# Two transformer blocks on one core: a chunked scan run as a pipeline over pairs of heads, and a last linear turned to rows

## What is computed

```python
def _wkv7_scan(r, w, k, v, a, b):
    def step(S, inp):
        r_t, w_t, k_t, v_t, a_t, b_t = inp
        sa = jnp.einsum('bhvk,bhk->bhv', S, a_t)
        S = (S * w_t[:, :, None, :] + sa[..., None] * b_t[:, :, None, :]
             + v_t[..., None] * k_t[:, :, None, :])
        return S, jnp.einsum('bhvk,bhk->bhv', S, r_t)
...
def _layer(h, ...):
    proj = _rms(h, n1) @ w_in
    z_rwkv, z_fox, z_gate = jnp.split(proj, (RWKV_COLS, RWKV_COLS + FOX_COLS), axis=-1)
    z_prev = jnp.pad(z_rwkv, ((0, 0), (1, 0), (0, 0)))[:, :-1]
    z_rwkv = z_rwkv + (z_prev - z_rwkv) * mu
    y_a = _rwkv7(z_rwkv, ...)        # r, k, v, decay, a, gate from z_rwkv, then the scan
    y_b = _fox(z_fox, q_g, k_g, f_bias)
    ...
    gate, up = jnp.split(_rms(h, n2) @ w_gu, 2, axis=-1)
    return h + (jax.nn.silu(gate) * up) @ w_dn
...
return h[:, N_META:]                 # the meta tokens are dropped
```

## Time and profile before

| | us |
|---|---|
| median of 3 runs | 2893.81 (2892.56 to 2895.17) |
| the profiled execution | 2892.87 |
| its span, first to last instruction | 2890.8 |
| TensorE busy | 2856.2 (99%) |
| VectorE busy | 1735.4 (60%) |
| ScalarE busy | 1223.3 (42%) |
| the scan with the side slots in it (first `sums` to last output of pair 8) | about 1398 to 1757 |
| `down2` | about 2633 to 2891 |

### The profile page before, as it was taken

How to read it: one execution, slowest core, us unless ns; L and a number is a source line. 1 busy time by engine, 2 the same in 40 slices (tenths; PEclk the granted TensorE clock), 3 DMA queues, 4 the chain that set the end, 5 groups by cost and what they waited for, 6 DMA issues and landing times.

```text
span 2890.8 us, 55153 instructions
## 1 busy us (share of the span) xinstructions
PE 2856.2 (99%) x23517; PEld 2629.2 (91%) x23517; DVE 1735.4 (60%) x2522; ACT 1223.3 (42%) x1788; POOL 53.0 (2%) x102
## 2 busy tenths in 40 slices
PE   9999999999999999999999999999999999999999
PEld 8999998888888999899888888899998888889999
DVE  6467757656566444754666665766666566655444
ACT  5345544333333344633433333455453333334343
POOL 1000000000000000000000000000000000000000
PEclk9999999999999999999999999999999999999999
DMA  7666445565555555455434335445555555555553
GB/s 245 199 168 167 156 163 172 177 190 187 188 189 175 190 187 189 153 167 168 118 88 118 102 89 160 132 123 184 180 186 188 182 183 187 189 189 183 182 188 131
DMA packets 370328, 485.21 MB, mean 168 GB/s; under 512 B 12359, under 2 KB 181654, under 8 KB 370150
## 3 DMA queue, kind: packets, MB, share of 16 engines
q1 hardware_dynamic: 362752, 471.55, 51.6%
q0 software_dynamic: 4112, 7.88, 0.9%
q10 hardware_dynamic: 3302, 3.39, 0.4%
HBM read 475.76 MB, written 7.01 MB: 167 GB/s over the span
## 4 chain that ended last, share of the span: by engine, by line
PE 91%; DVE 6%; issue 1%; ACT 1%; DMA 1%; DVEq 0%; SPq 0%; ACTq 0%
PE psum L338 20%; PE psum L344 12%; PE psum L342 12%; PE psum L343 12%; PE psum L340 10%; PE psum L543 6%; PE psum L547 5%; PE psum L545 5%; DVE w_lo L328 2%; PE psum L1796 1%; DVE arena L716 1%; PE psum L1782 1%; DVE arena L704 0%; PE psum L2612 0%; DVE act L791 0%
## 5 line engine op out<-in xcount | busy, mean ns | idle before, releaser
L328 DVE TENSOR_TENSOR w_lo<-w_raw,w_hi 128x1024 fp32r<-128x1024 f32 x728 | 859.0, 1221 | 797.6 <-ACT w_hi L319 797.6
L319 ACT ACTIVATE w_hi<-w_raw 128x1024 fp32r<-128x1024 f32 x728 | 731.4, 1052 | 1161.8 <-PE psum L340 591.5
L338 PE MATMUL psum<-act,w_hi 128*128 128x512 f32 x2816 | 989.6, 394 | 8.9 <-issue 4.5
L342 PE MATMUL psum<-act,w_hi 128*128 128x256 f32 (+2 forms) x3024 | 854.7, 283 | 6.9 <-issue 4.5
L344 PE MATMUL psum<-act,w_lo 128*128 128x256 f32 (+2 forms) x3024 | 855.6, 283 | 0.0
L343 PE MATMUL psum<-act,w_hi 128*128 128x256 f32 (+2 forms) x3024 | 855.6, 283 | 0.0
L340 PE MATMUL psum<-act,w_lo 128*128 128x256 f32 x2816 | 790.7, 281 | 0.0
L338 PEld LDWEIGHTS psum<-act,w_hi 128*128 128x128 f32 x2816 | 529.6, 188 | 136.8 <-DVE w_lo L328 11.2
L342 PEld LDWEIGHTS psum<-act,w_hi 128*128 128x128 f32 (+1 forms) x3024 | 571.6, 189 | 11.3 <-issue 8.3
L344 PEld LDWEIGHTS psum<-act,w_lo 128*128 128x128 f32 (+1 forms) x3024 | 572.2, 189 | 0.0
L343 PEld LDWEIGHTS psum<-act,w_hi 128*128 128x128 f32 (+1 forms) x3024 | 568.4, 188 | 0.1
(11 more groups left out here) (391 smaller groups left out, 1584.8 us busy)
## 6 DMA issues: line engine op xcount, KB each, us to landing
w_raw<-w_in SPq DMA_DIRECT2D x128, 1024.0 KB, 5.7
w_raw<-w_down SPq DMA_DIRECT2D x88, 1024.0 KB, 5.0
w_raw<-w_gate_up SPq DMA_DIRECT2D x88, 1024.0 KB, 5.0
w_raw<-w_gate SPq DMA_DIRECT2D x44, 1024.0 KB, 5.2
w_raw<-w_up SPq DMA_DIRECT2D x44, 1024.0 KB, 5.2
w_raw<-w_out SPq DMA_DIRECT2D x16, 1024.0 KB, 5.0
w_raw<-w_o SPq DMA_DIRECT2D x16, 1024.0 KB, 5.0
w_raw<-w_branch_a SPq DMA_DIRECT2D x8, 1024.0 KB, 5.0
```

The lines of the kernel that those rows point to most:

```text
L319: nc.scalar.activation(w_hi[:, s % 2, 2 * h:2 * h + 2, 0:wd], w_raw[:, s % RAW, 2 * h:2 * h + 2, 0:wd], ACT.Copy).then_inc(hi_ready, 1)
L328: nc.vector.tensor_tensor(w_lo[:, s % 2, 2 * h:2 * h + 2, 0:wd], w_raw[:, s % RAW, 2 * h:2 * h + 2, 0:wd], w_hi[:, s % 2, 2 * h:2 * h + 2, ...
L338: pe.matmul(dst.rearrange("p (h n) -> p h n", h=2), w1, both_parts, start=first, stop=False, skip_group_check=True)
L342: pe.matmul(dst, w1, act_hi[:, k, tok], start=first, stop=False, skip_group_check=True)
```

## The change

- **Chunk steps move.** The chunk steps of pair j - 1 (`chunk_x`, `chunk_u`, `chunk_y`) run between the inverse's steps of pair j. Those of pair 7 stand behind the loop, with slots between them. What they read is doubled or moved for that: `toks_s`, `inv_ts`, `to_mids`, `from_mids` have two copies, and `ar` lies in `z`. The copy of u moves from VectorE to ScalarE.
- **Slots in groups.** Of a step's 31 slots 30 stand in five groups (4, 4, 8, 6, 8) in its first part, and one in the inverse.
- **Gram split.** The product of `bh` with the a half is made only for the blocks that the inverse reads (`near` and `far`: twelve of 32 x 32, four of 64 x 64, per step); its r half (`gram_r`) and the product of `kh` (`gram_k`) come after the inverse.
- **Slots behind the scan.** The loop's end has 8 + 1 + 1 + 2 + 1 + 1 + 2 + 8 = 24 slots where it had 8. `fox_pe`, whose code is the same, is left with 132 slots where it had 148.
- **Last linear by rows.** `rows_pe` takes the activations (128 tokens) as stationary and 512 output features as moving operand. The residual is the first product into each bank (`res` times the identity). `down2_add` and the transposes are gone.
- **Narrow tiles.** The first 8 tiles of `rkv` (r) are made for 258 tokens and the first 8 of `fox` (q) for 256, both 272 before.

```diff
+        def rows_pe(lin, lo_base):
...
+            def residual(s):
+                for b in range(2):
+                    for j in range(4):
+                        pe.matmul(psum[:, 2 * s + b, j * P:(j + 1) * P],
+                                  res[:, 4 * s + j, META + b * P:META + (b + 1) * P], ident,
+                                  start=j == 0, stop=False, skip_group_check=True)
...
+                    if first:
+                        if s < 2:
+                            pe.wait_ge(acc_free, lin.t0 - 2 + 2 * s)
+                        residual(s)
+                    pe.wait_ge(lo_ready, 2 * u + 2)
+                    for b in range(2):
+                        out_rows = psum[:, 2 * s + b, :]
+                        half = slice(META + b * P, META + (b + 1) * P)
+                        for k in range(UNIT_K):
+                            w1, w0 = w_hi[:, s % 2, k], w_lo[:, s % 2, k]
+                            x1, x0 = act_hi[:, 4 * slot + k, half], act_lo[:, 4 * slot + k, half]
+                            pe.matmul(out_rows, x1, w1, start=False, stop=False, skip_group_check=True)
+                            pe.matmul(out_rows, x1, w0, start=False, stop=False, skip_group_check=True)
+                            mm = pe.matmul(out_rows, x0, w1, start=False, stop=last and k == UNIT_K - 1,
+                                           skip_group_check=True)
...
+        R_TOK = slice(META - 2, TOK)
+        def r_tiles(lin, i):
+            return lin is L["rkv"] and isinstance(i, int) and i < 2
...
+        def fox_tok(t):
+            return X if t < 8 else ALL
...
                 dve("n8t")
+                act("raw0")
                 product(4, n8t, n8, "p2")
-                gram(0, 0)
+                if j:
+                    chunk_x(before, 0)
                 dve("ip2")
                 product(5, ip2, i8t, "r1t")
                 act("p2")
                 product(4, p2t, p2, "p4")
-                gram(0, 1)
+                if j:
+                    chunk_u(before, 0)
                 dve("ip4")
                 act("r1t")
                 product(4, r1t, ip4, "s8")
-                gram(1, 0)
+                if j:
+                    act("near")
+                    chunk_y(before, 0)
                 dve("s8t")
                 product(5, nm16, s8t, "v16")
-                gram(1, 1)
+                side(1)
                 act("v16")
                 product(4, v16, s8, "s16")
-                side(1)
+                if j:
+                    chunk_x(before, 1)
                 dve("s16t")
                 product(5, nm32, s16t, "v32", 4)
-                side(1)
+                if j:
+                    chunk_u(before, 1)
                 act("v32")
                 product(4, v32, s16, "s32", 4)
-                side(1)
+                if j:
+                    chunk_y(before, 1)
...
+            side(8)
+            pe.wait_ge(*rd.after(("gram_k", 7)))
+            center(6)
+            chunk_x(7, 0)
+            side(1)
+            chunk_u(7, 0)
+            side(1)
+            chunk_y(7, 0)
+            side(2)
...
-            down_pe(L["down2"], LO_BASE["down2"], lambda s: s > 1 and end_transpose(s - 2))
-            end_transpose(2)
-            end_transpose(3)
+            rows_pe(L["down2"], LO_BASE["down2"])
```

## The result

The changed kernel takes 2920.1 us (median of 4 runs, 2912.9 to 2935.6) where the kernel before takes 2893.2: ratio 1.0096, 95% interval 1.0071 to 1.0121. That is 27 us slower; 2889.9 was forecast, and the range ended at 2901. The profiled execution has 2919.0 us and a span of 2916.9, 26.1 more than before.

A forecast was written before the change was run, and what follows sets the result against it. The kernel was taken as a queue of TensorE work. Narrow tiles -5.3, last linear -1.9, scan -6.3, fox attention's end +8.1 and clock +1.5 sum to -3.9 us, so 2889.9 us; 8 in 10 range 2874 to 2901.

The forecast's parts named there:

- the paragraph on the clock: Fox attention's end: half clock follows the new 5.3 us wait before pair 6's output, +1.5 us, from 0 to 3.5.
- the pair's walk: Scan, inverse and chunk steps: visits -2.7, gaps +0.9, tile changes +0.4, gram +0.1; net -1.3 us a pair.
- wait of 0.35 at x64t: Scan, inverse of a pair: only x0 stands behind v64, so TensorE waits 0.35 us at x64t.
- -8.9 was forecast: First `front` to `ysum`, less the moved slots: scan -6.3 us and `q` tiles -2.6.
- about 311 us: Scan: seven pairs from `sums` to `sums` should take about 311 us where they take 318.
- Rival 3: Inverse of pairs 1 to 7: chain of waits, 0.15 us more per step, 2902; chance 0.21 together with no pipeline gain.
- If a pair takes more than 46 us: Scan: one of the signs named in advance by which the prediction falls.
- the end of the fox attention: Behind the scan: 16 fewer slots for `fox_pe` bring waits of 5.3, 1.7, 0.4 and 1.3 us, less visits; +8.1 us.
- The 1.3 that was to come at the second weight unit: After `branch_first`: ScalarE, running later, and VectorE's part make TensorE wait 1.3 us for the second weight unit.
- the last linear: `down2` and tail: stream -5.4, residual +7.1, transposes in the stream -1.8, tail -1.8; sum -1.9 us.
- rival 2: `down2`: 512 wide matmuls run faster next to each other, 0.216 us, -17 us, 2873; chance 0.11.
- the narrow tiles: r tiles in `rkv` and q tiles in the scan's slots: fewer columns in 384 + 384 matmuls, -5.3 us.

The follow-up runs named there:

- a_spread: The changed kernel with 8 of a pair's 31 slots put back between the inverse's steps, in groups of 2, 3, 2, 2; 2894.0 us, 1.0002.
- b_narrow: The kernel before with the narrow tiles alone; 2890.5 us, 0.9984.
- a_rows128: The changed kernel with 16 of the 18 small matmuls of a product step using all 128 input rows against a fixed table; 2922.2 us, 1.0098.
- a_mid: The changed kernel with two of the eight slots before the inverse moved into the one visit in it, making three there; 2912.6 us, 1.0066.
- a_shift128: The changed kernel with 128 already satisfied waits put once into TensorE's program ahead of the scan; 2912.4 us, 1.0072.
- a_shift64: The changed kernel with 64 already satisfied waits put once into TensorE's program ahead of the scan; 2922.5 us, 1.0094.
- a_again: The changed kernel itself measured once more, as a control; 2924.6 us, 1.0106.

## Why the prediction was right or wrong

**Wrong: the clock.** The step that failed is the paragraph on the clock. It read from rows 8 that a wait of 4.8 us is followed by a stretch at half clock and one of 2.6 us isn't, priced the clock for the one new wait of 5.3 us alone (+1.5), and put it at nothing in the scan. Neither wait of rows 8 stands among small products. In the scan a gap of 1.9 us was enough, with small products around it, and the half clock then lasted 17 and 20 us. The fall of rows 8 lasts 6.8, of which 4.9 lie behind the wait. I had counted the 15 slots that leave the inverse as 2.7 us of visits saved. They also were what kept the clock up. Putting 8 of the 31 back between the steps (a_spread) took off 26 us: some 5 of them are the gaps' own length, the rest, some 21, is the clock.

**Missed: the instruction supply.** The walk of the pair took waits for VectorE and ScalarE only. The kernel before has issue gaps too, five at one line, 2.6 us in all, and one of 0.7 at another; I passed over them. Taking the slots away puts the small products closer together, and the gaps grow to 8.2 us in all (9.6 with that of pair 2). They add 5 to 6 us themselves, and the long falls of pairs 1 and 3 begin with them.

**Near: the pair's walk.** The pairs of the changed kernel at full clock (2, 4, 5 and 6) take 42.8 to 45.3 us, 44.1 on average, where they took 45.4 before. That is the 1.3 that was forecast, but with 0.7 of issue gaps in it, so the walk itself was too pessimistic by some 0.7 us a pair. Its wait of 0.35 at x64t isn't in the trace: in pair 2 x64t starts at 1532.47, 0.03 behind the end of x0. The waits of pair 0 are there, six of 0.4 us instead of four of 0.5. In a_spread the stretch from the first `front` to `ysum`, less 16 slots, is 362.2 against 371.2 before: -9.0, where -8.9 was forecast for the changed kernel. That they agree is partly luck. a_spread has 24 more visits (4.6 us at 0.19 each), and its slots cover waits that the walk had counted. The "about 311 us" for seven pairs also left out that the chunk steps of one of them move out of the stretch (4.2 us by the prediction's own figures) and that the `q` tiles are narrower; a_spread has 306.5. Rival 3 named the right place and direction, with the wrong mechanism: in the pairs at full clock no wait for a late copy shows. "If a pair takes more than 46 us" was the right alarm; two took 53 and 55.

**Right in its waits, partly lucky in its size: the end of the fox attention.** Forecast +8.1 and +1.5 for the clock, measured +11.0 alone and +11.4 in place. The two waits for ScalarE were 4.9 and 1.5 (forecast 5.3 and 1.7), the third 0.3 (0.4). The 1.3 that was to come at the second weight unit doesn't show, and the clock cost more than 1.5: two stretches at half clock, of 6.8 and 3.4 us, of which TensorE worked for 7.7, so up to some 4 us. The timelines of the changed kernel, TensorE and ScalarE, answer to rows 7:

```profile
1972.19 1.12 PE L2846 MATMUL psum<-arena 16*64 16x256 f32 x4 [4.89 <-ACT arena L2721]
...
1978.80 0.65 PE L2846 MATMUL psum<-arena 16*64 16x256 f32 x4 [1.46 <-ACT arena L2715]
...
1980.57 0.58 PE L342 MATMUL psum<-act,w_hi 128*128 128x256 f32 x1 [0.33 <-DVE act L833]
```
```profile
1971.57 0.57 ACT L2721 ACTIVATE arena<-psum 16x512 f32<-16x512 f32 x1
```

**Right within the noise: the last linear.** Forecast -1.9, measured -2.9 in place and -2.3 alone, where the interval reaches from -4.3 to +1.2. The change in `down2`, on TensorE and then at the end on VectorE:

```profile
2661.54 1.95 PE L695 MATMUL psum<-tab,res 128*128 128x128 f32 x16
...
2663.57 0.40 PE L717 MATMUL psum<-w_lo,act 128*128 128x512 f32 x1
2663.80 0.39 PE L718 MATMUL psum<-w_hi,act 128*128 128x512 f32 x1
2664.03 0.40 PE L716 MATMUL psum<-w_hi,act 128*128 128x512 f32 x1
```
```profile
2913.11 0.39 PE L718 MATMUL psum<-w_hi,act 128*128 128x512 f32 x1
2913.53 0.69 DVE L2944 COPY arena<-psum 128x512 f32<-128x512 f32 x1 [4.86 <-PE psum L718]
```

The wide matmuls start 0.23 us apart next to each other, so the row of `ffn` was the right base and rival 2 is out. 16 residual passes take 1.7 us in each of four units, 6.8 for the 7.1 in all. The copy starts 0.4 behind the last matmul.

**Right within the noise: the narrow tiles.** -3.7 alone for -5.3, which the interval (-7.2 to -2.0) holds. The half in `rkv` came out (-2.6 for -2.7). Of the half in the slots, the seven pairs of b_narrow show 2.1: 316.1 us for 318.2.

**Missed, small: the output steps.** TensorE's waits there for the gate weights grew from 2.3 to 3.0 us, and 3.4 us ran at half clock; together +2.3, which I had at nothing.

## What to carry to other kernels

Full matmuls strewn between small ones do two jobs that no wait in the profile shows: they give the instruction supply time, and they keep the clock. Before you group them, look in the trace for gaps put down to "issue" among the small matmuls, and leave two or three whole slots every few steps; a visit costs 0.19 us, and a stop with the fall behind it cost 9 to 11 us a pair. When pairs that do the same work take different times, look for what differs in place, not in work.

## What the runs showed of the hardware that I had not expected

- The granted clock fell, and stayed down, while TensorE was busy; in 13 of 24 cases no stop of 0.15 us or more was within 12 us before. Slots that fed 32 or 64 of the array's 128 rows, between small products, were followed by 31 to 48 us at 0.50 in every pair; slots that fed 128 rows and 32 columns by none in the scan, at equal instruction counts (3047.0 and 3034.9 against 2891.3 us). In the changed kernel, where the slots are whole, more input rows in the products changed nothing (a_rows128).
- TensorE stopped for up to 3.0 us (a_mid; 2.85 in the changed kernel) in the middle of 36 equal small matmuls, with no wait in the program. The stop moved when 64 or 128 instructions were added far ahead of it, once.
- Such a stop alone does not decide: 1.98 us in one pair (a_shift128) and 1.95 in another (a_shift64) had no fall behind them, 1.87 in a third had. Nor does the program: in pair 7 of the changed kernel and of a_again, which are the same, the stop stands at the same matmul (1.9 and 2.0 us) and was followed by 3.4 + 3.4 and by 17.1 us at half clock. What tips it is still open; I have no run that varies the gap alone.
